# Two down projections with joined column tiles, attention scores in rounded parts, decay arguments in rounded parts

## The reference, cut to what matters

```python
def mixer_block(x, ...):                     # 16 heads of 64: neighbourhood attention, beside a gated MLP branch
    s = einsum('bhrcd,bhrikd->bhrcik', qg, k_blk) * scale + bias
def conv_ffn(x, g_norm, w_up, conv_k, conv_b, w_down):
    h = rms_norm(x, g_norm)
    up = h @ w_up                            # 2048 x 11008
    up = three-tap convolution over the tokens, per column
    gate, val = jnp.split(up, 2, axis=-1)
    return x + (jax.nn.silu(gate) * val) @ w_down     # 5504 x 2048
def gated_deltanet(...):                     # second block, first layer
    diff = gc[..., :, None] - gc[..., None, :]        # gc: running sum of the log decay in a chunk
    decay = exp(where(tri_incl, diff, -inf))
```

## Time and profile before

| | |
|---|---|
| time, median of 3 runs | 2291.66 us (2291.44 to 2291.88) |
| profiled execution | 2291.97 us, its span 2290.2 us |
| TensorE busy | 2283.1 us of the span, 11199 products |
| VectorE, ScalarE, GpSimd busy | 1462.8, 1342.2, 70.3 us |
| granted TensorE clock | 1.000 over the span |

### The profile page before, as it was taken

One profiled execution on the slowest core, in us unless ns is written; L12 is line 12 of the kernel. 1 busy time (PEld: TensorE's weight loads), 2 busy tenths in 40 slices (PEclk: granted clock), 3 DMA queues, 4 the chain that ended last, 5 costly groups with the idle time before them and its releaser, 6 DMA issues.

```text
span 2290.2 us, 29601 instructions
## 1 busy us (share of the span) xinstructions
PE 2283.1 (100%) x11199; PEld 1887.1 (82%) x11199; DVE 1462.8 (64%) x2019; ACT 1342.2 (59%) x1974; POOL 70.3 (3%) x94
## 2 busy tenths in 40 slices
PE   9999999999999999999999999999999999999999
PEld 7887778888888888888888888888888888888887
DVE  5757555556666665466766677787977665555554
ACT  5557564444566564365665576667674556566653
POOL 0011100000200000000000001010000000000000
PEclk9999999999999999999999999999999999999999
DMA  8789996667888876588886756675755788977974
GB/s 269 219 264 264 262 247 219 215 214 216 255 246 237 241 230 200 178 253 236 246 235 196 241 158 199 172 212 164 228 157 177 223 258 228 259 223 227 265 223 164
DMA packets 463678, 510.61 MB, mean 223 GB/s; under 512 B 188305, under 2 KB 284337, under 8 KB 463409
## 3 DMA queue, kind: packets, MB, share of 16 engines
q1 hardware_dynamic: 457408, 500.30, 74.4%
q10 hardware_dynamic: 6128, 8.43, 1.1%
HBM read 428.94 MB, written 45.89 MB: 207 GB/s over the span
## 4 chain that ended last, share of the span: by engine, by line
PE 95%; DVE 2%; ACT 1%; DVEq 1%; DMA 0%; issue 0%; ACTq 0%
PE gemm L777 30%; PE gemm L778 29%; PE gemm L779 29%; DVE w_lo L748 1%; PE aux L779 1%; PE aux L778 1%; PE aux L777 1%; PE aux L2450 1%; ACT w_hi L738 1%; PE aux L2859 0%; PE aux L2845 0%; PE aux L2640 0%; PE aux L2528 0%; PE aux L2545 0%; PE aux L2652 0%
## 5 line engine op out<-in xcount | busy, mean ns | idle before, releaser
L748 DVE TENSOR_TENSOR w_lo<-raw,w_hi 128x1024 fp32r<-128x1024 f32 (+1 forms) x800 | 953.2, 1205 | 552.9 <-ACT w_hi L738 548.4
L738 ACT ACTIVATE w_hi<-raw 128x1024 fp32r<-128x1024 f32 (+1 forms) x800 | 817.5, 1039 | 485.2 <-PE gemm L779 341.8
L777 PE MATMUL gemm<-w_lo,hT 128*128 128x512 f32 x2304 | 903.0, 392 | 1.5 <-DVE hT L1651 0.9
L779 PE MATMUL gemm<-w_hi,hT 128*128 128x512 f32 x2304 | 893.8, 388 | 0.0
L778 PE MATMUL gemm<-w_hi,hT 128*128 128x512 f32 x2304 | 893.7, 388 | 0.0
L777 PEld LDWEIGHTS gemm<-w_lo,hT 128*128 128x128 f32 x2304 | 432.8, 188 | 95.1 <-issue 4.7
L779 PEld LDWEIGHTS gemm<-w_hi,hT 128*128 128x128 f32 x2304 | 432.6, 188 | 89.6
L778 PEld LDWEIGHTS gemm<-w_hi,hT 128*128 128x128 f32 x2304 | 432.9, 188 | 85.6 <-issue 0.2
L777 PE MATMUL gemm<-w_lo,yT_hi 128*128 128x512 f32 x472 | 184.3, 391 | 0.1
L779 PE MATMUL gemm<-w_hi,yT_lo 128*128 128x512 f32 x472 | 183.7, 389 | 0.0
L778 PE MATMUL gemm<-w_hi,yT_hi 128*128 128x512 f32 x472 | 183.6, 389 | 0.0
(11 more groups left out here) (347 smaller groups left out, 1804.1 us busy)
## 6 DMA issues: line engine op xcount, KB each, us to landing
raw<-in_w_up SPq DMA_DIRECT2D x336, 256.0 KB, 3.7
raw<-in_w_in SPq DMA_DIRECT2D x144, 512.0 KB, 4.9
raw<-in_a_w_in SPq DMA_DIRECT2D x128, 512.0 KB, 4.1
raw<-in_b_w_in SPq DMA_DIRECT2D x128, 512.0 KB, 4.5
raw<-in_w_down SPq DMA_DIRECT2D x76, 512.0 KB, 4.5
raw<-in_w_branch SPq DMA_DIRECT2D x32, 512.0 KB, 5.2
raw<-in_w_out SPq DMA_DIRECT2D x32, 512.0 KB, 4.4
raw<-in_a_w_out SPq DMA_DIRECT2D x32, 512.0 KB, 4.4
```

The source lines that it names most:

```text
L738: nc.scalar.activation(hi, src, ACT.Copy).then_inc(S("hi_done"), 1)
L748: nc.vector.tensor_tensor(lo, src, hi.bitcast(F32), ALU.subtract).then_inc(S("lo_done"), 1)
L777: nc.tensor.matmul(dst, xh, wl[:, k, :], start=h["start"] and k == 0, stop=False)
L779: mm = nc.tensor.matmul(dst, xl, wh[:, k, :], start=False, stop=h["stop"] and k == h["n"] - 1)
```

## The change

- In each down projection the first two column tiles are joined: all loads but the last of tile 0, all but the last of tile 1, then the last load of tile 0, the last of tile 1, then tiles 2 and 3 as before.
- The last up tile is turned by DMA like the others: planes written ahead of the eighth half's load of tile 0, transpose behind the second load of tile 1. TensorE's transposes and ScalarE's copies out of PSUM are gone.
- In the second group all residual pieces are turned within tiles 2 and 3: piece 0 is written ahead of the fourth load of tile 2 and transposed behind the sixth; piece 1 is written ahead of the twelfth and transposed behind the second load of tile 3; piece 2 is written ahead of the seventh load of tile 3 and transposed behind the ninth. Before the last two transposes SyncE also waits until VectorE has used the piece before (`stage_free`).
- The neighbourhood scores become three rounded products each, of `qT` and `kT` split into rounded part and remainder by ScalarE and VectorE (four of each). The second keys are turned one load earlier.
- The arguments of the decay become products of rounded parts, two in place of each full one; VectorE makes the parts.
- The bias copies from memory to memory go out in 16 pieces of one head, one every third half, in place of four of four heads; the mixing weights are loaded 16 halves later and split later.

```diff
     parts += [(FOUR, "h", 0, 512)] * UP1 + [(DOWN1, "y", 0, 512)] * 4
+    downs = [(len(parts) - 4, DOWN1)]
     parts += [(FOUR, "h", 0, 256)] + [(FOUR, "h", 0, 512)] * (UP2 - 1) + [(DOWN2, "y", 0, 512)] * 4
+    downs += [(len(parts) - 4, DOWN2)]
 
     parts = [(t, *p, True, True) for t, p in enumerate(parts)]
+    for t, loads in downs[::-1]:
+        parts[t:t + 2] = ([(t + j, loads[:-1], "y", 0, 512, True, False) for j in range(2)]
+                          + [(t + j, loads[-1:], "y", sum(loads[:-1]), 512, False, True) for j in range(2)])
     for _ in range(2):
         t = parts[-1][0] + 1
...
-    return n + (UP1 - 1 if j0 else 0)
+    return j0 + n
...
                         sp.wait_ge(S("conv_val_done"), buf - 1)
-                return dict(before={1: keep}, ready={4: ready}, behind={4: lambda: turn_planes(ut[buf % 2], 4 + c % 2, "up_turned")})
+                return dict(before={at: keep}, ready={to: ready}, behind={to: lambda: turn_planes(ut[buf % 2], 4 + c % 2, "up_turned")})
+
+            def down_tiles(loads, k0, j0, tiles, third={}, fourth={}):
+
+                first, second = up_turn(j0, tiles - 2), up_turn(j0, tiles - 1, 7, 1)
+                first["before"] = {**first["before"], **second.pop("before")}
+                for i in range(2):
+                    tile("down", loads[:-1], i * 512, k0, **(second if i else first))
+                for i in range(2):
+                    tile("down", loads[-1:], i * 512, k0 + sum(loads[:-1]))
+                tile("down", loads, 2 * 512, k0, **third)
+                tile("down", loads, 3 * 512, k0, **fourth)
 
             def load_bias(u, j):
 
                 a, h = j // 2, j % 2
...
-            sp.dma_start(wsT[:, :, :], ins["gm_w_s"]).then_inc(S("consts_landed"), 16)
-            sp.dma_start(bsT[:, :], ins["gm_b_s"]).then_inc(S("consts_landed"), 16)
-            tile("in", [4, 4], GMW + 512, 8)
...
-            for j in range(4):
-                tile("in", [4], 512, 4 * j)
+            tile("in", [4, 4], 512)
+            sp.dma_start(wsT[:, :, :], ins["gm_w_s"]).then_inc(S("mix_landed"), 16)
+            sp.dma_start(bsT[:, :], ins["gm_b_s"]).then_inc(S("mix_landed"), 16)
+            tile("in", [4, 4], 512, 8)
             for g in range(2):
...
                     tile("up", FOUR, n * 256, **(up_turn(0, n - 2) if n >= 2 else {} if n else turn_rows(X_TURNS[1] + 2, 0)))
-                for i in range(4):
-                    tile("down", DOWN1, i * 512, **({} if i else up_turn(0, UP1 - 2)))
+                down_tiles(DOWN1, 0, 0, UP1)
                 for n in range(UP2):
                     tile("up", FOUR, n * 256 + UP1 * 256 - (P if n else 0), width=512 if n else 256, **(up_turn(UP1, n - 2) if n >= 2 else {}))
-                for i in range(4):
-                    tile("down", DOWN2, i * 512, 2 * UP1, **(turn_rows(X_TURNS[2] + i - 1, 8) if i else up_turn(UP1, UP2 - 2)))
+                x_turns = [turn_rows(X_TURNS[2] + j, at) for j, at in enumerate((3, 11, 6))]
+
+                def stage_free(j, ready):
+
+                    sp.wait_ge(S("hT_lo_done"), 8 * 2 + 2 * j)
+                    ready()
+                third = dict(before={**x_turns[0]["before"], **x_turns[1]["before"]},
+                             ready=x_turns[0]["ready"], behind=x_turns[0]["behind"])
+                fourth = dict(before=x_turns[2]["before"],
+                              ready={1: lambda: stage_free(1, x_turns[1]["ready"][13]), 8: lambda: stage_free(2, x_turns[2]["ready"][8])},
+                              behind={1: x_turns[1]["behind"][13], **x_turns[2]["behind"]})
+                down_tiles(DOWN2, 2 * UP1, UP1, UP2, third, fourth)
...
+            def hi_of_rows(n, dst, src):
+                act.wait_ge(S("qk_turned"), 32 * (n + 1))
+                A(dst[:, :, :], src[:, :, :], ACT.Copy).then_inc(S("qk_hi"), 1)
+
...
 
                 for step in range(55):
+                    if step == 26:
+                        hi_of_rows(2, qT_hi, qT)
+                    for n, at in enumerate((0, 28)):
...
-            mix = mixing()
+            def bias_copies():
+                for h in range(NAH):
+                    copy_bias(na_skew, ins["na_rpb"], SKEW, f"na_copied{h // 4}", h, 1)
+                    yield
+                    yield
+                    yield
+
+            mix, copies = mixing(), bias_copies()
...
                 yield
 
-            def up_side(j0, n, last=False):
+            def up_side(j0, n):
 
                 blk0, kt, w = up_blocks(j0, n)
+                last = n == (UP2 if j0 else UP1) - 1
                 n, c = j0 + n, up_dma(j0, n)
                 gate, val, sums = cg[n % 2], cv[n % 2], ut[n % 2]
-                for _ in range(3 if last else 1):
-                    yield
-                if last:
-                    act.wait_ge(S("up_last_turned"), j0 // UP1 + 1)
-                    act.wait_ge(S("conv_val_done"), n - 1)
-                    for b in range(2):
-                        A(sums[:, 2 * b:2 * b + 2, :], AX[b][:, :].rearrange("p (a t) -> p a t", a=2), ACT.Copy)
-                    act.drain()
-                else:
-                    act.wait_ge(S("up_turned"), 16 * (c + 1))
+                for _ in range(4 if last else 1):
+                    yield
+                act.wait_ge(S("up_turned"), 16 * (c + 1))
...
-                run(half, 2 * len(loads) - 1, up_side(j0, tiles - 2), up_side(j0, tiles - 1, True))
-                for s in range(3):
-                    run(half, 2 * len(loads), down_x(s, T_DOWN2 + s) if j0 else none)
+                run(half, 2 * len(loads) - 3, up_side(j0, tiles - 2), up_apart(j0, tiles - 1, t0 + tiles - 1))
+                run(half, 2 * len(loads) - 2, up_side(j0, tiles - 1))
+                run(half, 2)
+                turns = [down_x(s, T_DOWN2 + s, 6 if s == 1 else 0) if j0 else none for s in range(3)]
+                run(half, 2, turns[0])
+                run(half, 2 * len(loads), turns[0], turns[1])
...
                                     ALU.subtract).then_inc(S("yb_lo"), 1)
 
                 for step in range(55):
+                    if step == 27:
+                        lo_of_rows(2, qT_lo, qT, qT_hi)
+                    for n, at in enumerate((0, 29)):
+                        if step == at:
...
                     up_read(t0 + n, j0, n)
-                run(half, 2 * len(loads) - 1, up_side(j0, tiles - 2), up_side(j0, tiles - 1, True))
+                run(half, 2 * len(loads) - 3, up_side(j0, tiles - 2))
+                run(half, 2 * len(loads) - 2, up_side(j0, tiles - 1))
+                run(half, 2)
+                turns = [down_x(s, 6 if s == 1 else 0) if j0 else none for s in range(3)]
                 add_tile(t_down, 0)
-                for s in range(1, 4):
-                    run(half, 2 * len(loads), down_x(s - 1) if j0 else none)
-                    add_tile(t_down + s, s * 512)
+                run(half, 2, turns[0])
+                add_tile(t_down + 1, 512)
+                run(half, 2 * len(loads), turns[0], turns[1])
+                add_tile(t_down + 2, 1024)
+                run(half, 2 * len(loads), turns[1], turns[2])
+                add_tile(t_down + 3, 1536)
 
...
-                for tb in range(TB):
-                    e = V.tensor_tensor(dec[:, tb * HG:(tb + 1) * HG, :], rep(m_le[:, :], HG), each(gg[:, tb, 0:HG], P), ALU.mult)
+                V.tensor_copy(m_gt_r[:, :], m_gt[:, :])
+                V.tensor_copy(gg_parts[:, 0, :, :], gg[:, :, 0:HG])
+                dve.drain()
+                V.tensor_tensor(gg_parts[:, 1, :, :], gg[:, :, 0:HG], gg_parts[:, 0, :, :].bitcast(F32), ALU.subtract)
+                dve.drain()
+                for part in range(2):
+                    if part:
+                        yield
+                    for tb in range(TB):
+                        e = V.tensor_tensor(arg_parts[part][:, tb * HG:(tb + 1) * HG, :], rep(m_le[:, :], HG),
+                                            each(gg_parts[:, part, tb, :].bitcast(F32), P), ALU.mult)
                 e.then_inc(S("d_gm"), 1)
-                yield
                 yield
                 dve.wait_ge(S("gc_done"), 1)
...
                         for tb in range(TB):
-                            for a in range(2):
-                                rows_ = slice(a * NAD, (a + 1) * NAD)
-                                m = MM(score_banks(u % 2)[a][:, tb * T:(tb + 1) * T], qT[rows_, u % 4, tb * P:(tb + 1) * P],
-                                       kT[rows_, u % 4, :], start=True, stop=True)
-                                if tb:
-                                    m.then_inc(S("na_scores"), 1)
+                            for part, (q_part, k_part) in enumerate(((qT_lo, kT_hi), (qT_hi, kT_lo), (qT_hi, kT_hi))):
+                                for a in range(2):
+                                    rows_ = slice(a * NAD, (a + 1) * NAD)
```

(15 more changed lines are left out.)

111 lines of the change are left out of this document (66 added, 45 removed).

## The result

The changed kernel takes 2297.52 us (median of 14 runs, 2295.74 to 2298.95), the kernel before 2291.58 (2291.44 to 2292.62, 14 runs). The ratio is 1.0025, with a 95% interval of 1.0017 to 1.0032: 5.9 us slower. The forecast was 2296.3 in a range of 2288.5 to 2302.5. One run of the kernel before, among the 33 beside the first four experiments, took 6490.71 us and is left out.

A forecast was written before the change was run, and what follows sets the result against it. TensorE bounds the kernel, busy 2283.1 of 2290.2 us. Transposes -1.8, decay -0.7, scores -1.3, old stalls -0.4, up-tile holds +0.9 and residual holds +7.9 sum to +4.6 us: 2296.3, range 2288.5 to 2302.5.

The forecast's parts named there:

- five places: Down projections: SyncE stands still before weight loads; 0.9 us for the last up tile's two, 7.9 for the three residual pieces.
- the first residual piece: Second group, tile 2: its write and transpose hold SyncE, so TensorE waits 2.0 us for the seventh half.
- The second transpose: Second group, second residual piece: its transpose delays the third load of tile 3, 2.2 us of wait.
- D8: Ninth half of tile 3, second group: load waits until VectorE has used the second piece; 1.1 us of wait.
- D9: Tenth half of tile 3, second group: load comes behind the third piece's transpose; 2.6 us of wait.
- A7: Eighth half of tile 0, second group: its load stands behind the last up tile's plane write; 0.3 us of wait.
- B2: Third half of tile 1, second group: its load stands behind the last up tile's transpose; 0.5 us of wait.
- the fifth place: Third residual piece, second group, tile 3: waits of 1.1 us at the ninth half and 2.6 at the tenth.
- nothing, bound 1 us: Scores: the added roundings and subtractions on ScalarE and VectorE cost nothing, since both run several us ahead; bound 1 us.
- (a): Second group's loads in tiles 2 and 3: SyncE's holds are hidden, waits 0 to 4 us, 2287.5 to 2291.5; chance 0.26.
- (b): Neighbourhood scores: rounded products on the two 64-row halves don't overlap, +5.5 us over the forecast, 2301.8; chance 0.17.
- (c): Neighbourhood stage: VectorE becomes the bound, a late half costing 1 to 2 us, inside the range; no chance of its own.

The follow-up runs named there:

- the first four experiments: Changed kernel without the second group's join, 2291.78 us; kernel before plus only both joins, 2296.80, only scores and front, 2291.06, or only decay, 2292.85.
- joins alone: The kernel before with both down projections' joins and nothing else of the change; 2296.80 us, ratio 1.0022.
- the kernel with the short stall: Changed kernel with holds moved later and old decay arguments; first group's fourth load of tile 3 waits until TensorE finishes tile 2; 2291.43 us.
- the middle stall: Changed kernel, holds later, old decay arguments; first group's fourth load of tile 3 waits until TensorE finishes that tile's first half; 2293.72 us.
- the long one: Changed kernel, holds later, old decay arguments; first group's fourth load of tile 3 waits until TensorE finishes that tile's second half; 2295.87 us.

## Why the prediction was right

**The mechanism.** It stood: an engine's queue, SyncE's, was made to stand still in front of weight loads, and five places were named. For the first residual piece the count from A11's end on TensorE (1243.68) came out closely. Forecast and measured: write of the planes at 3.7 and 3.6, C3's load at 4.1 and 4.1, C6's load at 12.9 and 12.8, ready at 19.7 and 19.8, stall 2.0 and 1.84. Two errors cancel in it: the write landed in 3.1 us (taken 4.4), and the transpose held SyncE for 5.5 (taken 4.3).

**The other places.** The second transpose held 3.0 us, the write ahead of it landed in 3.0. So D2's load left 31.7 us after A11, not 34.3, and the half was ready at 1282.6, 0.1 ahead of its turn: no stall, where 2.2 were forecast. This is the term that was mis-sized most; one median duration was put into a chain of several, where each hold varied from 3.0 to 5.5. D8 was 1.20 (1.1), D9 1.32 (2.6; the transpose took 3.5). A7 was 0.92 (0.3). TensorE was due there 1.2 us earlier than counted, having gained in the first group too, but the load also left 1.2 us earlier (1198.93 for 1200.1), so that cancels. The stall grew because the load landed in 5.3 us behind the write (taken 4.9), and TensorE began 7.75 us after it left (taken 7.2). B2 was 0 (0.5), its transpose took 3.3. The first group's two places stayed near nothing. All five together are 5.3 us in the profiled execution, forecast 8.8. The forecast's own count has a slip in the fifth place: with 4.3 us to land and 2.4 of rounding, a load that leaves at 51.0 is ready at 57.7 and not at 57.0, which would give 1.8 and 2.0 us where it has 1.1 and 2.6; the sum is the same to 0.1.

**What TensorE was spared.** Eight transposes, twice: the first group ends 1.2 us ahead with the front's 0.2, so 0.9 as counted. Scores: 0.31 a burst, forecast 0.3, and overlap was the right choice; what was wrong is "nothing, bound 1 us" for VectorE's share, about 0.6 by the medians and 1.1 in the traces. Decay: TensorE gains 0.46 us over that stage in place of 0.7. The block itself takes 1.04 us (1381.20 to 1382.24), as forecast, with 0.34 for the first of its four products, on top of 0.26 for the way in.

**What was missing.** The decay's VectorE work was put at nothing with a bound of 0.5, with the reason that it lies a few halves ahead of its use. Its use was not what mattered: the copy behind it was. Alone, the part costs 1.1 us where 0.7 of gain were forecast. The second miss is that TensorE's clock takes its share after a long stall, in some runs: two of the changed kernel's 14 have a mean granted clock of 0.999 (2298.49 and 2298.62 us); which stall stood ahead of it there, no trace shows. The third concerns a sign that the forecast named for being wrong, gaps in the neighbourhood stage. Two came, of 0.55 us at 216.10 and 0.51 at 274.49 (at 216.21 before, 0.38; at the second place before, none over 0.11). They are small against the 5.3 us, but they are there.

**The sum.** In the profiled execution the forecast's +4.6 stands against +4.7. Its stalls were 3.5 us too high. What made up for it: the decay part, +0.65 in place of -0.7; scores and front, -0.2 in place of -1.3; 0.7 in C and D beside the stalls themselves (behind each the next product comes after 0.34 instead of 0.227, and C4 and C5 came just in time); 0.3 outside the span. So the nearness of the sum is partly luck. By the medians it is +5.9. The changed kernel and "joins alone" spread by about 3 us and stall by 5.3 and 6.6 us in their traces. The lowered clock is a part of that spread, in two runs of 14 and three of 11. It is not all of it: the slowest run of the changed kernel (2298.95) has a mean clock of 1.000, and so has every run of the kernel with the short stall, which spreads by 2.4 us. That the stalls themselves change in length from run to run is likely and not shown, since each kernel has one trace.

**The rivals.** (a), holds hidden, fell: "joins alone" is at +5.1. It decides where it was said to: with the holds one or two loads later the stalls go, and the kernel, with the old decay arguments, comes to -1.1. Of that way from +5.9, about 1.1 us is the decay part and the rest the holds. (b), no overlap, fell by the 0.12 us. (c), VectorE as the bound in the neighbourhood stage, did happen in part, at 0.6 us, inside the range. The Trainium skill, DMA: Bandwidth & Descriptors, Latency and other measured facts, gives a rate for DMA_TRANSPOSE by which 0.5 MB would take 2.0 us (an estimate from that page). The three of this stage held the queue for 3.0 to 5.5 us and landed 5.1 to 9.1 us after issue, beside weight loads, so the measurement decides against it here.

## What to carry to other kernels

A queue's hold costs nothing until it outlasts its lead, and then all that it is over; so where an order is changed, count for each hold the load behind it, its landing and its turn on the busy engine, and try the same hold one load later before giving the change up. Here that was worth some 6 of the 7 us between +5.9 and -1.1, the old decay arguments the rest. Against the kernel before, -1.1 us is within what the interval can't tell from none. And a chain of holds is to be counted with its shortest and its longest duration, not with the median.

Work on an engine with spare time is not free by its share: look at what stands behind it in that engine's order and who waits for that. A saving on the busy engine is lost when the next stage is paced by another: its slack there (0.2 to 0.6 us before, between a half's remainder and its first product) is the most that it can give.

## What the hardware showed

In the profiled executions TensorE went on at full clock after stalls of 1.55 and 1.84 us. After 2.40, 2.5 and 3.88 us its products were 0.43 us apart for six, seven and eleven distances (the granted clock of 0.50 is the 1.2 GHz level), and then came back to 0.23. By the records the stall of 2.40 us thus cost 4.0 in all and that of 3.88 us 6.4. The clock does not fall in every execution: behind the middle stall six runs of 11 show it in their mean, behind the long one eight, in "joins alone" three. The Trainium skill, TensorE: Matmul & The Clock Gate, Part 1, gives a start-to-start distance of N divided by 1.2 GHz for the lower level, 426.7 ns for 512 columns; the rows agree.

The same transpose DMA of 0.5 MB held SyncE's queue between 3.0 and 5.5 us within one stage of one execution.
